# The causal mask of the forgetting attention: from 16 mask products on the matmul array to GpSimd selects in the gates' running sums, with the query blocks taken from last to first

## The reference, cut to what matters

```
log_f = log_sigmoid(fx_f + b_forget)
dcum  = cumsum(log_f, axis=1)                       # per head, over the tokens
logits = q @ k * scale + dq[:, None] - dcum[None, :]   # dq is dcum at the query
logits = where(kpos <= qpos, logits, -inf)
p = softmax(logits);  y_fox = p @ v
```

## Time and profile before

| what | value |
|---|---|
| median of three runs | 710.95 us |
| the profiled execution | 711.37 us |
| its span, first to last instruction | 709.5 us |
| mean granted clock of the array | 0.995 of full |
| PE busy | 690.8 us, 97% |
| VectorE busy | 373.2 us, 53% |
| ScalarE busy | 254.5 us, 36% |
| GpSimd busy | 91.3 us, 13% |

### The profile page before, as it was taken

How to read it: one execution, slowest core, us unless ns; L and a number is a source line. 1 busy time by engine, 2 the same in 40 slices (tenths; PEclk the granted TensorE clock), 3 DMA queues, 4 the chain that set the end, 5 groups by cost and what they waited for, 6 DMA issues and landing times.

```text
span 709.5 us, 10025 instructions
## 1 busy us (share of the span) xinstructions
PE 690.8 (97%) x3923; PEld 508.0 (72%) x3923; DVE 373.2 (53%) x732; ACT 254.5 (36%) x423; POOL 91.3 (13%) x130
## 2 busy tenths in 40 slices
PE   8999999999999999999999999999999999999894
PEld 7888988777777777788888888666555556555442
DVE  5378996666676868556446214752513121212227
ACT  7332133587676777544244211220101111111113
POOL 2000922000000101100003000011311312131100
PEclk9999999999999999999999999999999999999998
DMA  7523244322222111493406699699999999999993
GB/s 241 177 61 118 61 127 143 139 75 75 75 75 74 48 59 49 162 385 113 136 2 237 225 382 346 268 353 387 405 417 420 403 419 418 419 419 417 419 394 134
DMA packets 60585, 164.58 MB, mean 232 GB/s; under 512 B 8090, under 2 KB 39911, under 8 KB 48116
## 3 DMA queue, kind: packets, MB, share of 16 engines
q1 hardware_dynamic: 54820, 151.77, 56.3%
q0 software_dynamic: 5712, 12.11, 4.6%
HBM read 155.68 MB, written 16.00 MB: 242 GB/s over the span
## 4 chain that ended last, share of the span: by engine, by line
PE 89%; DVE 4%; DMA 3%; ACT 1%; issue 1%; POOL 0%; SPq 0%; POOLq 0%; DVEq 0%; ACTq 0%
PE psum L1749 31%; PE psum L2175 14%; PE psum L1848 12%; PE psum L2201 8%; PE psum L2028 6%; PE psum L1860 3%; PE psum L2141 2%; DVE ring_e L1105 2%; DMA ring_e<-y_dram 2%; PE psum L1873 1%; PE psum L1904 1%; PE psum L2184 1%; DMA y_dram<-ye,slots_b 1%; PE psum L1987 1%; PE psum L1939 1%
## 5 line engine op out<-in xcount | busy, mean ns | idle before, releaser
L1749 PE MATMUL psum<-xh,wh 128*128 128x512 f32 x256 | 99.9, 390 | 0.8 <-DVE xl L1105 0.8
L1749 PE MATMUL psum<-xl,wh 128*128 128x512 f32 x256 | 99.6, 389 | 0.0
L1749 PE MATMUL psum<-xh,wl 128*128 128x512 f32 x256 | 99.6, 389 | 0.0
L1108 DVE TENSOR_TENSOR wl<-raw,wh 128x1280 fp32r<-128x1280 f32 (+4 forms) x37 | 71.8, 1945 | 24.6 <-ACT wh L801 9.0
L1105 DVE SCALAR_TENSOR_TENSOR hid<-psum,rslot,act_g 128x256 f32<-128x256 f32 x17 | 8.2, 483 | 92.3 <-PE psum L2175 91.7
L1749 PEld LDWEIGHTS psum<-xh,wh 128*128 128x128 f32 x256 | 48.1, 188 | 11.0 <-DVE xl L1105 1.0
L1749 PEld LDWEIGHTS psum<-xh,wl 128*128 128x128 f32 x256 | 48.1, 188 | 10.0
L1749 PEld LDWEIGHTS psum<-xl,wh 128*128 128x128 f32 x256 | 48.1, 188 | 9.8
L1848 PE MATMUL psum<-xh,wh 128*128 128x512 f32 x128 | 51.3, 401 | 0.0
L1848 PE MATMUL psum<-xh,wl 128*128 128x512 f32 x128 | 50.1, 391 | 0.0
L1848 PE MATMUL psum<-xl,wh 128*128 128x512 f32 x128 | 49.9, 390 | 0.0
(11 more groups left out here) (388 smaller groups left out, 1531.6 us busy)
## 6 DMA issues: line engine op xcount, KB each, us to landing
raw<-in_w_gate SPq DMA_DIRECT2D x16, 1024.0 KB, 6.3
raw<-in_w_in SPq DMA_DIRECT2D x9, 1024.0 KB, 5.5
ring_w<-in_w_expert_gate SPq DMA_DIRECT2D x8, 1024.0 KB
ring_w<-in_w_expert_up SPq DMA_DIRECT2D x8, 1024.0 KB
ring_h<-in_w_expert_down SPq DMA_DIRECT2D x8, 1024.0 KB
ring_h<-in_w_expert_gate SPq DMA_DIRECT2D x6, 1024.0 KB
ring_e<-in_w_expert_down SPq DMA_DIRECT2D x6, 1024.0 KB
ring_e<-in_w_expert_gate SPq DMA_DIRECT2D x6, 1024.0 KB
```

The lines of the kernel that those rows point to most:

```text
L1108: return dve.tensor_tensor(dst, src, hi.bitcast(F32), ALU.subtract)
L1749: last = nc.tensor.matmul(dst, a, b, start=start and n == 0, stop=stop and n == len(seq) - 1)
```

## The change

- `fox_step` goes through the query blocks of each head from last to first: qt = 3 - n % 4, so m is 512, 384, 256, 128. The stick-breaking widths stay 128, 256, 384, 512.
- maskb, its memset and its select at the start, and the 16 products of L1908 go.
- GpSimd writes 2^100 into the 128x128 block of dcum that belongs to the step's own queries, above the diagonal (`later_keys`). VectorE's pass over the forgetting scores then subtracts it. The block of step n + 1 is written after VectorE has read the row of step n. It is written in place, and a query block with fewer keys never reads the blocks to its right, which is why the order is from last to first.
- VectorE waits for the select of its step; the semaphore `consts` is renamed `made` and counts these too.
- The signal that the forgetting scores are complete now comes from their last score product.

```diff
         def fox_step(n):
-            return fox_head(n // NT), n % NT, (n % NT + 1) * P
+            qt = NT - 1 - n % NT
+            return fox_head(n // NT), qt, (qt + 1) * P
...
+            def later_keys(n):
+
+                h, qt, m = fox_step(n)
+                select(dcum, P, ALU.is_ge, -MASKED, 0, -1, 1, dcum[:, h, m - P:m]).then_inc(S["made"], 1)
+
+            pool.wait_ge(S["dc_in"], 16)
+            later_keys(0)
             for n in range(STEPS):
                 h, kt, q0 = stick_step(n)
+                if n + 1 < STEPS:
+                    pool.wait_ge(S["l_max"], n + 1)
+                    later_keys(n + 1)
                 if kt == 0:
                     continue
...
                         dve.wait_ge(S["pt_psum"], n)
+                    dve.wait_ge(S["made"], n + 2)
                     st.link(dve.tensor_tensor_reduce(out=lg[:, 0:m], in0=bank[1][:, 0:m], in1=dcum[:, h, 0:m], scale=1.0,
...
-                        nc.tensor.matmul(bank[1][:, 0:m], ql[r2:r2 + HD, j2, qt * P:(qt + 1) * P], kl[r2:r2 + HD, j2, 0:m], start=i == 0, stop=i == 2)
+                        last = nc.tensor.matmul(bank[1][:, 0:m], ql[r2:r2 + HD, j2, qt * P:(qt + 1) * P], kl[r2:r2 + HD, j2, 0:m], start=i == 0, stop=i == 2)
+                    last.then_inc(S["l_psum"], 1)
                     nc.tensor.matmul(bank[0][:, q0:q0 + P], identb[:, :], cutb[:, :], start=False, stop=True,
                                      skip_group_check=True).then_inc(S["z_psum"], 1)
-                    nc.tensor.matmul(bank[1][:, m - P:m], identb[:, :], maskb[:, :], start=False, stop=True,
-                                     skip_group_check=True).then_inc(S["l_psum"], 1)
                     gates(BEHIND_SCORES)
```

More of the change, by code:

```diff
@@ L128, in hybrid_trunk @@
         neg_one = sb(main, "neg_one", [P], F32R)
-        maskb = sb(main, "maskb", [P], BF16)
         strictb = sb(main, "strictb", [P], BF16)
@@ L304, in hybrid_trunk @@
         S = {name: sem(name) for name in (
-            "pool_step act_step dve_step consts small_in tabs_ready x0 x1 x2s x3 sq_done root xn_ready "
+            "pool_step act_step dve_step made small_in tabs_ready x0 x1 x2s x3 sq_done root xn_ready "
             "xt_psum hi_out xt_ready raw0 raw1 rest0 rest1 hi_ready split_ready unit_used "
@@ L653, in _ @@
             for t, v in ((ident, 0.0), (causal, 1.0), (tri_made, -1.0), (one_made, -1.0),
-                         (maskb, 0.0), (cutb, 0.0), (strictb, 1.0), (oneb, 1.0), (eps, EPS)):
+                         (cutb, 0.0), (strictb, 1.0), (oneb, 1.0), (eps, EPS)):
                 st.mark(pool.memset(t[:], v))
@@ L664, in _ @@
             st.mark(select(tri_made, P, ALU.is_ge, 0.0, 0, -1, 1))
-            st.mark(select(maskb, P, ALU.is_ge, MASKED, 0, -1, 1))
             st.mark(select(cutb, P, ALU.is_gt, MASKED, 0, 1, -1))
@@ L669, in _ @@
             st.link(pool.tensor_copy(identb[:, :], ident[:, :]))
-            pool.sem_inc(S["consts"], 1)
+            pool.sem_inc(S["made"], 1)
             evacuated(pool, "ac")
@@ L808, in _ @@
                 if t == 0:
-                    act.wait_ge(S["consts"], 1)
+                    act.wait_ge(S["made"], 1)
                 act.activation(stat[:, 1, t:t + 1], stat[:, 0, t:t + 1], ACT.Sqrt, bias=eps[:, 0:1], scale=1.0 / D).then_inc(S["root"], 1)
@@ L1179, in _ @@
             split_lo(1, KC * PROJ[1][2])
-            dve.wait_ge(S["consts"], 1)
+            dve.wait_ge(S["made"], 1)
             st.mark(dve.tensor_copy(causal_r[:, :], causal[:, :]))
@@ L1754, in _ @@
                 nc.tensor.matmul(bank[3][:, 0:P], pt[:, 0, :], pt[:, 1, :], start=True, stop=True)
-            pe.wait_ge(S["consts"], 1)
+            pe.wait_ge(S["made"], 1)
             for t in range(NT):
```

## The result

| | before | after |
|---|---|---|
| median | 711.11 us (9 runs, 709.54 to 713.17) | 716.65 us (9 runs, 714.37 to 718.07) |
| ratio of the runs | | 1.0064, 95% interval 1.0043 to 1.0084 |
| the profiled execution, span | 709.5 us | 714.8 us |
| the loop, first score product to first gate product behind the last products with v | 150.87 us | 155.62 us |
| ahead of the loop | 144.35 us | 144.34 us |

The kernel is slower by 0.64% (0.43 to 0.84), 4.6 us on 711.11; the two medians are 5.5 us apart, inside that interval's 3.1 to 6.0. In the profiles the loop grows by 4.75 us, and the rest of the program keeps its length to 0.6 us. The windows show it: the first line is the loop in the profile before, the three behind it are the profile after, cut at the loop's ends.

A forecast was written before the change was run, and what follows sets the result against it. The matmul array was taken to bound the loop; scores +2.36, products with v +3.48, mask products -1.12 and the loop's end -0.2 gave +4.5 us, so 715.5 us from a median of 710.95, range 712.3 to 717.3.

The forecast's parts named there:

- The array bounds the loop, and the loop's change arrives at the end: Matmul array in the loop: waits only once, 0.2 us, so added array time is carried to the end in full.
- Score products by the wider half: Score products in the loop: each unequal pair costs what its wider half costs, +0.59 us a head, +2.36 us in all.
- Products with v by the wider half: Products with v in the loop: each pair costs its wider half, +0.87 us a head, +3.48 us in all.
- Mask products: Removed L1908 products, 16 at 0.07 us each between score products and gate product: -1.12 us (-0.5 to -1.6).
- The end of the loop: Last products with v: narrower forgetting block shortens the chain to the copy of pt, the array's wait goes, -0.2 us.
- VectorE, ScalarE, the selects and the wait on them: nothing: Other engines in the loop: work stays hidden behind the array, some 0.4 us left in tightest step 0, no time change.
- Hidden surplus: Rival, products with v: wider half's surplus overlaps the next instructions, only scores pay; +1.0 us, 712.0; chance 0.13.
- The mean of the widths: Rival, half-array pairs: a pair costs the mean of its widths, -1.8 us in sum, 709.2; chance 0.08.
- One after the other: Rival, half-array pairs: unequal halves run serially, +14.4 us in sum, 725.4; chance 0.05.
- The vector chain: Rival, VectorE against GpSimd selects: chain grows 1 us, array waits 0.6 in step 0, 716.1; inside the forecast's 0.74.

The follow-up runs named there:

- e3: Kernel after, with forgetting score products as wide as the stick-breaking ones beside them (result wrong); loop 153.53 us, ratio to before 1.0038.
- e4: Kernel after, with as many forgetting products with v as fit the stick-breaking width beside them (result wrong); loop 152.19 us, ratio to before 1.0012.
- e6: Kernel before, with each of the 16 mask products issued five times; loop 154.26 us against 150.87, ratio to before 1.0042.
- e1: Kernel before, with only the forgetting query blocks reversed, mask products kept, no selects in dcum; loop 156.40 us, ratio to before 1.0066.
- e5: Kernel after, with each select in dcum done four times; loop 155.61 us against 155.62, ratio to before 1.0061.
- e7: Kernel before, with a step's three stick-breaking score products issued first, then the three forgetting ones; loop 150.96 us, ratio to before 1.0009.

## Why the prediction was right

The forecast was 715.5 us (712.3 to 717.3), 4.5 us more than before; the median is 716.65. By the ratio of the runs the kernel lost 4.6 us, by the loop 4.75. That the two medians lie 5.5 apart is within the interval of the nine runs.

- *The array bounds the loop, and the loop's change arrives at the end.* Right. In the kernel after the array waits 0.2 us in the loop; the loop grew by 4.75 us, the span by 5.3, the time by 0.64%, 4.6 us. The rest of the span, 0.6 us, lies after the loop, which varied by more than that between the profiled kernels.
- *Score products by the wider half, +2.36.* Right. The distances in a head were forecast as 0.90, 0.72, 0.72, 0.90 and are 0.89, 0.73, 0.73, 0.89 in the first. The 16 add up to 10.61 us before and 12.96 after, +2.35; taken out (e3) the loop falls by 2.09 with a new wait of some 0.2 in step 0.
- *Products with v by the wider half, +3.48.* Right, slightly too large. The 16 distances add up to 11.16 and 14.51, +3.35; e4 gives 3.43. A block of 512 columns beside one product takes 1.01, not the 1.03 of 512 beside four.
- *Mask products, -1.12.* The size was off: from cutb to the gate product the 16 steps take 1.52 us before and 0.63 after, 0.89 less or 0.056 each, as in e6; that is in the lower half of the bounds of 0.5 to 1.6. The forecast took the 0.07 between L1906 and L1908 for the price. What the loop gains is another distance, that from L1906 to the gate product: it averages 0.095 before and 0.039 after.
- *The end of the loop, -0.2.* Wrong. The wait went from 0.25 to 0.17. Counted from the last step's first transpose (291.90 before, 297.06 after), the copy of pt ends after 2.24 us before and after 1.85, 0.39 earlier. But the transposes went from four to one, and the gate products behind them start after 0.41 before and after 0.09, so the array comes 0.32 earlier too. The forecast counted the one and not the other.
- *VectorE, ScalarE, the selects and the wait on them: nothing.* Right, with the margin as forecast: 0.37 us left in step 0, 0.4 forecast. e3 shows that it was close, since 0.4 us less on the array were enough to make it wait.
- The sum of what was measured, 2.35 + 3.35 - 0.89 - 0.08, is 4.73, the loop measures 4.75. A head became 1.21 us longer (37.67 to 38.88, second head), 1.18 forecast. That the forecast's 4.5 came so near is in part luck: the cost of the products with v was put 0.13 too high, the gain of the masks 0.23 and that of the end 0.12, and the first error stood against the other two.
- *The rivals.* Hidden surplus (712.0): refuted by e4, 3.43 us. The mean of the widths (709.2): refuted by e1 and e3. One after the other (725.4): refuted by the profile after. The vector chain: not the bound (e5).
- *The two pages.* The Trainium skill (TensorEngine Tiling (Array Packing), section Tiling Modes) has tiles operate independently and a change of the tiling mode drain the array. The traces agree in kind: narrow products ran on beside a wide one (182.37 beside a wide one from 182.09 to, as modelled, 182.59), and the full-array product, at 183.00, did not start before the wider half was through. That it is the drain which holds it was not tried apart from its need of all rows. The Trainium skill (SBUF — State Buffer, section Who interferes with whom) has VectorE and GpSimd shut each other out. The copy of 0.48 us and VectorE's 0.37 in e5 fit it in kind; no run here tells exclusion for the whole length of an instruction from a milder slowing.

## What to carry to other kernels

Where two chains of products share the array by halves, count the columns of each half between two full-array instructions; here the stretch cost what the larger count costs. Reordering one chain of the pair is not free even if its own work stays the same: here it cost 5.5 us (e1) to save 0.9. If a trick demands another order (an in-place mask that a later step must not see), look first whether an idle engine can undo it; GpSimd had room for a save and a restore in each step, and that version kept the widths and the saving.

## What the runs showed of the hardware

- The order of issue inside a stretch of half-array score products (64 rows each) hardly mattered: three products of one half and then three of the other took 0.90 us at 512 columns, as in turn (e7). I had assumed independence from one row; that a half can be three instructions ahead in the program was more than I expected.
- A bf16 product of 128 columns with a 128x128 identity, behind another of its kind, costs the array 0.056 us (e6: 3.58 us for 64, from cutb to the gate product).
- The same 2379 array instructions after the loop took 414.84 us at a granted clock of 0.99 and 416.64 at 0.98 (after and e5), so the time of one run says less about a change of this size than the length of the loop does.
